# Memory products ahead of the token rows' normalisation, in one step of a hybrid decoder on one core

## The reference, cut to what matters

```python
xp = layer_norm(x_prompt, ln_in_g, ln_in_b)      # (512, 1024)
xs = layer_norm(x_sample, ln_in_g, ln_in_b)      # (8, 1024)
mkv = mem_prompt @ w_mem_kv                      # (256, 1024) @ (1024, 512): memory keys and values
z = x @ w_in                                     # x: the 520 normalised rows; 22 column tiles of 128, then 24 gate tiles
...                                              # RWKV time mixing, window attention, memory attention, gates
x1 = layer_norm(ALPHA * x + mix, ln1_g, ln1_b)
x2 = layer_norm(ALPHA * x1 + experts(x1), ln2_g, ln2_b)   # 32 experts, 2 per row

def layer_norm(x, g, b):
    mu = mean(x); var = mean((x - mu)**2)
    return (x - mu) * rsqrt(var + eps) * g + b
```

## Time and profile before

| | us |
|---|---|
| runs | 1454.42, 1457.96, 1458.41 (median 1457.96) |
| the profiled execution | 1459.9 |
| its span, first to last instruction | 1458.1 |
| TensorE busy in the span | 1163.3 (80%) |
| VectorE, ScalarE, GpSimd busy | 433.6, 239.1, 110.1 |
| mean granted clock of TensorE | 0.907 |

### The profile page before, as it was taken

The page is one execution under the profiler, slowest core; times in us unless marked ns, Lnnn a source line. Parts: engine busy times, 40 slices in busy tenths (PEclk is TensorE's granted clock), DMA queues, the critical chain, the costliest instruction groups (busy, mean ns, idle before and its releaser), DMA issues.

```text
span 1458.1 us, 22199 instructions
## 1 busy us (share of the span) xinstructions
PE 1163.3 (80%) x9283; PEld 808.1 (55%) x9283; DVE 433.6 (30%) x775; ACT 239.1 (16%) x400; POOL 110.1 (8%) x97
## 2 busy tenths in 40 slices
PE   5999989985896887898699971977878878878840
PEld 3888867774575776786585431544434434444420
DVE  5000022447464443443432236111111111111137
ACT  3100010432411111012111110211111111111101
POOL 3000000000000000000000111111111111111103
PEclk9999989998798999999799975999999999999975
DMA  7352341223033101105456222699999999999951
GB/s 265 116 149 77 76 151 45 66 65 87 1 85 85 41 29 29 43 10 182 126 152 243 109 107 62 237 427 426 425 425 419 422 416 410 421 420 420 423 216 74
DMA packets 102114, 290.91 MB, mean 200 GB/s; under 512 B 18067, under 2 KB 73429, under 8 KB 88714
## 3 DMA queue, kind: packets, MB, share of 16 engines
q1 hardware_dynamic: 96866, 281.41, 50.9%
q0 software_dynamic: 5184, 8.54, 1.7%
HBM read 274.97 MB, written 24.23 MB: 205 GB/s over the span
## 4 chain that ended last, share of the span: by engine, by line
PE 57%; DMA 25%; DVE 8%; issue 4%; SPq 2%; DVEq 2%; ACT 2%; POOL 0%; POOLq 0%; ACTq 0%
PE psum L660 54%; DMA arena<-in_e_up 12%; DMA arena<-in_e_gate 8%; DVE arena L1432 4%; PE psum L665 3%; DVE arena L1435 2%; DMA arena<-in_p_m 1%; ACT arena L1197 1%; DMA arena<-in_w_mem_kv 1%; DMA arena<-scratch_x,arena 1%; DVEq L1586 1%; SPq L584 0%; SPq L641 0%; DVEq L2014 0%; POOL arena L2027 0%
## 5 line engine op out<-in xcount | busy, mean ns | idle before, releaser
L660 PE MATMUL psum<-arena 64*64 64x64 f32 (+8 forms) x8760 | 1089.1, 344 | 178.2 <-DMA arena<-in_e_gate 61.2
L660 PEld LDWEIGHTS psum<-arena 64*64 64x64 f32 (+3 forms) x8760 | 744.9, 155 | 500.1 <-issue 251.6
L1197 ACT ACTIVATE arena<-psum 128x512 f32<-128x512 f32 (+8 forms) x151 | 94.8, 648 | 693.2 <-PE psum L660 385.8
L1432 DVE TENSOR_TENSOR arena<-arena,psum 128x256 f32<-128x256 f32 (+3 forms) x136 | 74.4, 548 | 398.3 <-PE psum L660 199.4
L1432 DVE TENSOR_TENSOR arena<-arena 128x1024 f32<-128x1024 f32 (+15 forms) x148 | 122.7, 840 | 210.5 <-PE psum L660 164.3
L665 PE MATMUL psum<-arena 128*128 128x128 f32 (+4 forms) x523 | 84.6, 302 | 64.3 <-issue 15.6
L665 PEld LDWEIGHTS psum<-arena 128*128 128x128 f32 (+4 forms) x523 | 63.6, 159 | 96.8 <-issue 65.1
L2027 POOL TENSOR_TENSOR arena<-arena 128x1024 f32<-128x1024 f32 (+1 forms) x15 | 37.1, 2476 | 578.7 <-DVE arena L1432 578.7
L1432 DVE TENSOR_TENSOR arena<-psum,arena 128x256 f32<-128x256 f32 (+5 forms) x85 | 47.4, 566 | 108.6 <-PE psum L660 107.6
L2070 POOL DMA_INDIRECT arena<-scratch_x,arena x32 | 32.8, 1024 | 300.2 <-DVE arena L1965 299.6
L1410 ACT ACTIVATE arena<-psum 128x256 f32<-128x256 f32 x32 | 12.3, 384 | 252.9 <-PE psum L660 252.9
(11 more groups left out here) (105 smaller groups left out, 155.3 us busy)
## 6 DMA issues: line engine op xcount, KB each, us to landing
arena<-in_e_gate SPq DMA_DIRECT2D x32, 2048.0 KB, 16.8
arena<-in_e_up SPq DMA_DIRECT2D x32, 2048.0 KB, 21.9
arena<-in_e_down SPq DMA_DIRECT2D x32, 2048.0 KB, 12.6
arena<-in_w_in SPq DMA_DIRECT2D x24, 512.0 KB, 4.6
arena<-in_w_in SPq DMA_DIRECT2D x44, 256.0 KB, 3.4
scratch_gates<-arena SPq DMA_DIRECT2D x24, 260.0 KB, 4.6
arena<-scratch_gates SPq DMA_DIRECT2D x8, 780.0 KB, 5.0
scratch_x<-arena SPq DMA_DIRECT2D x8, 512.0 KB
```

Of the source, the lines that this page charges most:

```text
L660: return pe.matmul(out, a, b, start=start, stop=stop)
L1197: return act.activation(out, a, ACT.Copy)
L1432: return v.tensor_tensor(out, a, b, op)
```

## The change

The memory is given transposed (`mem_T`, partition p holds the features 8p to 8p+7 for all 256 memory rows, 1024 KB), and the norm's weight and bias also as columns (`ln_in_T`, 64 bytes for each partition, 8 KB). SP's order becomes: `memT`, identity, lower half of `w_mem_kv`, row tile 0, its upper half, row tiles 1 to 4, `lnT`, the first two tiles of `w_in`, then the spread weight and bias, the constants and the rest. The queues of PE, ACT and DVE stand in this order in the diff below. TensorE makes the lower half of all memory products first, turns row tile 0, makes the upper half, and turns tiles 1 to 4. Rows are turned when scaled, without weight and bias; these are applied where the turned tile is evicted, columns 0 to 3 on DVE and 4 to 7 on ACT, one instruction a column, with weight and bias of a partition as operands. The weight and bias of the rows in `xtok` follow later (DVE, then POOL). ACT copies `mkv` after the last eviction of rows, and `mkT` is made after the tiles of `z`.

```diff
-            x_load(0)
+            sp.dma_start(memT, I["mem_T"]).then_inc(s["mem_in"], 16)
             sp.dma_start(view(C0, P + 2), I["consts"][:, 0:P + 2]).then_inc(s["ident_in"], 16)
-            sp.dma_start(gb[:, 0, :], I["ln_in_g"].partition_broadcast(P)).then_inc(s["x_in"], 16)
-            sp.dma_start(gb[:, 1, :], I["ln_in_b"].partition_broadcast(P)).then_inc(s["x_in"], 16)
-            x_load(1)
-            sp.dma_start(memtok, I["mem_prompt"].rearrange("(t p) d -> p t d", p=P)).then_inc(s["mem_in"], 16)
-            for t in range(2, Q):
-                x_load(t)
-            sp.dma_start(wmem, I["w_mem_kv"].rearrange("(p c) n -> p c n", c=KD)).then_inc(s["wmem_in"], 16)
+            sp.dma_start(wmem[:, 0:4, :], w_mem[:, 0:4, :]).then_inc(s["wmem_lo"], 16)
+            x_load(0)
+            sp.dma_start(wmem[:, 4:8, :], w_mem[:, 4:8, :]).then_inc(s["wmem_hi"], 16)
+            for t in range(1, Q):
+                x_load(t)
+            sp.dma_start(lnT, I["ln_in_T"]).then_inc(s["lnT_in"], 16)
+            p1_tile(0, 0, 1)
+            p1_tile(1, 1, 2)
+            sp.dma_start(gb[:, 0, :], I["ln_in_g"].partition_broadcast(P)).then_inc(s["x_in"], 16)
+            sp.dma_start(gb[:, 1, :], I["ln_in_b"].partition_broadcast(P)).then_inc(s["x_in"], 16)
...
             def turn_x(t):
-                pe.wait_ge(s["x_normed"], t + 1)
+                pe.wait_ge(s["x_scaled"], t + 1)
                 if t >= 2:
                     pe.wait_ge(s["xT_ready"], t - 1)
+                    pe.wait_ge(s["xT_half"], t - 1)
...
-            for t in range(2):
-                for c in range(KD):
-                    last = turn(bank(4 + 2 * t, KD, P)[:, c, :], memtok[:, t, c::KD])
-                last.then_inc(s["mem_turned"], 1)
-            pe.wait_ge(s["memT_ready"], 2)
-            pe.wait_ge(s["wmem_in"], 16)
...
+            for half in range(2):
+                pe.wait_ge(s["wmem_hi" if half else "wmem_lo"], 16)
                 for t in range(2):
+                    for c in range(half * 4, half * 4 + 4):
+                        last = mm(bank(4 + t, 512), memT[:, c, t * P:(t + 1) * P], wmem[:, c, :], c == 0, c == KD - 1)
+                    if half:
+                        last.then_inc(s["mkv_made"], 1)
+                if half == 0:
+                    turn_x(0)
+            for u in range(1, Q):
+                turn_x(u)
             pe.wait_ge(s["xT_ready"], Q)
+            pe.wait_ge(s["xT_half"], Q)
...
             def x_turned(t):
                 act.wait_ge(s["x_turned"], t + 1)
-                copy(xT[:, :, t * P:t * P + n], bank(2 * (t % 2), KD, P)[:, :, 0:n]).then_inc(s["xT_ready"], 1)
+                for c in range(KD // 2, KD):
+                    last = act.activation(xT[:, c, t * P:t * P + n], bank(2 * (t % 2), KD, P)[:, c, 0:n], ACT.Identity,
+                                          bias=lnT[:, 1, c:c + 1], scale=lnT[:, 0, c:c + 1])
+                last.then_inc(s["xT_ready"], 1)
+            act.wait_ge(s["lnT_in"], 16)
+            layer_norm(xtok, 0, 1, after=lambda t: x_turned(t - 2) if t >= 2 else None)
+            x_turned(Q - 1)
             for t in range(2):
                 act.wait_ge(s["mkv_made"], t + 1)
                 copy(mkv[:, t, :], bank(4 + t, 512)).then_inc(s["mkv_ready"], 1)
...
+            for t in range(Q + 2):
+                if t < Q:
+                    n = rows(t)
+                    v.wait_ge(s[f"tile{t}_in"], 16)
+                    for h in range(2):
+                        v.bn_stats(st6[0:n, t, h, :], xtok[0:n, t, h * 512:(h + 1) * 512])
+                    v.drain()
+                    v.bn_aggr(mv[0:n, t, :], st6[0:n, t, :, :]).then_inc(s["ln_stats"], 1)
+                u = t - 1
+                if 0 <= u < Q:
...
+                    v.reciprocal(rstd[0:n, u, :], rstd[0:n, u, :])
+                    v.drain()
+                    stt(nmr[0:n, u, :], mv[0:n, u, 0:1], -1.0, rstd[0:n, u, :], ALU.mult, ALU.mult).then_inc(s["ln_rs"], 1)
+                u = t - 2
+                if u >= 0:
+                    n = rows(u)
+                    v.wait_ge(s["x_turned"], u + 1)
...
+                    for c in range(KD // 2):
+                        last = ts(xT[:, c, u * P:u * P + n], bank(2 * (u % 2), KD, P)[:, c, 0:n], lnT[:, 0, c:c + 1], ALU.mult,
+                                  lnT[:, 1, c:c + 1], ALU.add)
+                    last.then_inc(s["xT_half"], 1)
+            v.wait_ge(s["x_in"], 32)
+            for t in range(Q):
+                n = rows(t)
+                tt(xtok[0:n, t, :], xtok[0:n, t, :], gb[0:n, 0, :], ALU.mult).then_inc(s["ln_gained"], 1)
```

More of the change, by code:

```diff
@@ L196, in build @@
         PRM = take(PR_N + 6)
+        LNT = take(2 * KD)
         GBo = take(2 * D)
@@ L216, in build @@
         gb = view(GBo, 2, D)
+        lnT = view(LNT, 2, KD)
         sm = [SMo]
@@ L245, in build @@
         xtok = view(Fo, NT + 1, D)
-        memtok = view(Fo + 5120, 2, D)
         memT = view(Fo + 7168, KD, NMEM)
@@ L434, in _ @@
             first = C0 + P + 2
[L435 to L449 removed]
             w_in = I["w_in"].rearrange("(p c) n -> p c n", c=KD)
+            w_mem = I["w_mem_kv"].rearrange("(p c) n -> p c n", c=KD)
             def p1_load(q, need, src_a, src_b, dst_a, dst_b):
@@ L468, in _ @@
             for f in range(2 * PIECES + 2):
-                p1_tile(f, f % 2, f + 1)
+                if f >= 2:
+                    p1_tile(f, f % 2, f + 1)
                 if f == 1:
@@ L715, in _ @@
                     last.then_inc(s["z_made"], 1)
+            pe.wait_ge(s["mkv_ready"], 2)
+            for f in range(2):
+                for t in range(2):
+                    last = turn(bank(6, 2, NMEM)[:, f, t * P:(t + 1) * P], mkv[:, t, f * P:(f + 1) * P])
+            last.then_inc(s["mkv_made"], 1)
             pe.wait_ge(s["z_ready"], NF + 2)
@@ L1201, in layer_norm @@
             def layer_norm(x, pas, lag, before=None, after=None):
+                scaled = s["x_scaled" if pas == 0 else "ln_scaled"]
                 for t in range(Q + lag):
@@ L1214, in layer_norm @@
                         act.activation(x[0:n, i, :], x[0:n, i, :], ACT.Identity, bias=nmr[0:n, i, :],
-                                       scale=rstd[0:n, i, :]).then_inc(s["ln_scaled"], 1)
+                                       scale=rstd[0:n, i, :]).then_inc(scaled, 1)
                     if after:
@@ L1234, in _ @@
                 copy(mkv[:, t, :], bank(4 + t, 512)).then_inc(s["mkv_ready"], 1)
[L1235 to L1238, removed]
             act.sem_inc(s["z_ready"], 2)
@@ L1244, in _ @@
                          psum[:, 2 * q:2 * q + 2, 0:NH]).then_inc(s["z_ready"], 1)
+            act.wait_ge(s["mkv_made"], 3)
+            copy(mkT, bank(6, 2, NMEM)).then_inc(s["mkT_ready"], 1)
             act.wait_ge(s["side_turned"], SIDE_PARAMS)
@@ L1462, in layer_norm @@
                         i, n = tile_at(pas, u), rows(tile_at(pas, u))
-                        v.wait_ge(s["ln_scaled"], pas * Q + u + 1)
+                        v.wait_ge(s["ln_scaled"], (pas - 1) * Q + u + 1)
                         tt(x[0:n, i, :], x[0:n, i, :], gb[0:n, 0, :], ALU.mult).then_inc(s["ln_gained"], 1)
[L1466 to L1471, removed]
+            for t in range(Q + 2):
[9 more added lines that the diff above has]
+                    n = rows(u)
+                    v.wait_ge(s["ln_std"], u + 1)
+                    v.reciprocal(rstd[0:n, u, :], rstd[0:n, u, :])
[3 more added lines that the diff above has]
+                if u >= 0:
+                    n = rows(u)
+                    v.wait_ge(s["x_turned"], u + 1)
+                    if u == 0:
+                        v.wait_ge(s["lnT_in"], 16)
+                    for c in range(KD // 2):
[6 more added lines that the diff above has]
+                tt(xtok[0:n, t, :], xtok[0:n, t, :], gb[0:n, 0, :], ALU.mult).then_inc(s["ln_gained"], 1)
             v.wait_ge(s["mkT_ready"], 1)
@@ L2131 @@
     give("x_sample", np.reshape(a["x_sample"], (B, D)))
-    give("mem_prompt", np.reshape(a["mem_prompt"], (NMEM, D)))
+    give("mem_T", np.transpose(np.reshape(a["mem_prompt"], (NMEM, P, KD)), (1, 2, 0)))
+    give("ln_in_T", np.stack([np.reshape(a[n], (P, KD)) for n in ("ln_in_g", "ln_in_b")], 1))
     give("state_wkv", np.reshape(a["state_wkv"], (B * HA, 64, 64)))
```

26 lines of the change are left out of this document (9 added, 17 removed).

## The result

The changed kernel takes 1466.59 us, median of 9 runs (1463.88 to 1471.13), against 1457.96 for 9 runs of the kernel before (1451.20 to 1463.04): ratio 1.0066, interval 1.0047 to 1.0086. It is slower, by about 8.6 us at the medians, and lies above the predicted 1460.4 us and above the range's upper end of 1464.5. The profiled execution took 1466.59 us with a span of 1464.7, 6.6 us over the span before.

A forecast was written before the change was run, and what follows sets the result against it. The prediction took the start and speed of `z`, behind `w_mem_kv` and the memory products, as the bound; -3.2 + 2.5 + 2.5 + 0.6 = +2.4 us on 1457.96 gave 1460.4 us, range 1454.5 to 1464.5.

The forecast's parts named there:

- the first one: Whole kernel: everything after `z` waits for it, so only when and how fast `z` begins matters; no size of its own.
- the rivals: Only the fall before `z`, 1457.9 us (0.22); faster head, down to 1452.9 (0.14); late `lnT`, 1462.4 to 1464.1 (0.18).
- Lower products at 9.0: Head, TensorE: lower weights land at 9.0 us, and the first half of the memory products ends at 18 to 19.
- `lnT` at 17.2: Head, load ACT first waits for: `lnT` lands at 17.2 us, between 16.0 and 18.4.
- Turning of tile 0 at 20.55: Head, TensorE: after `lnT`, table load, root, reciprocal and scaling, row tile 0 can be turned at 20.55 us.
- The fall before the upper half: Head: TensorE's pause of some 2 us drops its clock to 0.50, costing 2.5 us (zero to 3.1).
- the two readings of the transposes: Head clock: transposes don't count as work (skill's rule), making this fall sure, or do (rows), leaving a quarter chance of none.
- From T to `z`: Head, from tile 1 turned (T = 29.4 us) to `z`: alternating ACT and DVE work takes 11.1 us; `z` at 40.5, -3.2.
- The fall before `z`: Run-up to `z`: TensorE's pauses drop the clock to 0.50, all but certainly, costing 2.5 us (zero to 3.1).
- The tail of `z`: End of `z`: TensorE waits for the copy to `mkT` behind ACT's last eviction, +0.6 us (zero to 0.7).
- Sum of the head: All terms: -3.2 for `z` sooner, +2.5 and +2.5 for clock falls, +0.6 for the tail, together +2.4 us.

The follow-up runs named there:

- E5: The changed kernel with `lnT` loaded third instead of tenth and 32 do-nothing instructions at TensorE's head, later code in place: 1455.61 us, ratio 0.9990.
- E1: The changed kernel with 32 do-nothing instructions at TensorE's head, later code standing where the kernel before has it: 1457.06 us, ratio 0.9996.
- E2: The kernel before with only the memory given transposed and one do-nothing instruction, TensorE's later code 32 instructions lower: 1465.57 us, ratio 1.0049.
- E8: E6 with 97 instead of 33 do-nothing instructions at TensorE's head, later code 64 further on than in the kernel before: 1454.51 us, ratio 0.9992.
- E6: E5 plus three PSUM places, scaling before evictions, statistics before DVE's halves, turning between product quarters, `mkv` after `z_ready`; code in place: 1449.06 us, ratio 0.9936.

## Why the prediction was wrong

The step that failed is the first one: "What comes after `z` waits for it in every queue. So the question is when and how fast `z` begins." That the rest begins with `z` holds; that it then takes as long as before does not. In the profiles it took 7.4 us longer, and 8.1 us were lost in the time-mixing loop, code that the diff doesn't touch, because TensorE's program before it is 32 instructions shorter. Three pairs show it: the change with its code moved and in place (1.0066 against 0.9996 and 1.0016), the transposed memory alone (1.0049 against 1.0007), the three places in PSUM (0.9978 against 0.9936 and 0.9926), 4 to 7 per mille each time. None of the rivals had this, and none could be priced by the rows that I had read: they were of the head, of forms and of clocks.

The other steps, in their order:

- Lower products at 9.0: 8.48 us, ended at 18.1 (forecast 18 to 19). `lnT` at 17.2: 16.88. Turning of tile 0 at 20.55: 20.30. These were right.
- The fall before the upper half, 2.5 us: it came, at 20.39, and cost 1.8, as 1.97 + 7.91 us against E5's 1.05 + 7.04. It does not decide between the two readings of the transposes, for both had a fall here.
- From T to `z`, 11.1 us: 9.5, from 30.91 to 40.45. ACT's and DVE's evictions that it rests on:

```profile
30.91 1.51 ACT L1233 ACTIVATE arena<-psum,arena 128x128 f32<-128x128 f32 x4 [4.22 <-PE psum L672]
...
37.67 2.43 ACT L1233 ACTIVATE arena<-psum,arena 128x128 f32<-128x128 f32 x8
40.01 1.05 ACT L1205 ACTIVATE arena<-psum 128x512 f32<-128x512 f32 x2
```

```profile
30.91 1.36 DVE L1446 TENSOR_SCALAR arena<-psum,arena 128x128 f32<-128x128 f32 x4 [5.50 <-PE psum L672]
```

  Four columns took 1.51 on ACT (1.55 taken), the last eight 2.43 (2.75), four on DVE 1.36 (1.05). The `mkv` copies, for which the sum had 1.15 us, were not in the way: `z` began at 40.45, while they ran.
- The fall before `z`, 2.5 us: it came, and cost 156.59 - 154.72 = 1.9. The tail of `z`, +0.6: from the end of `z` to the side transposes 1.33 us instead of 0.79, +0.5.
- Sum of the head: +2.4 forecast; -0.8 in the profiles, for the `z` of 40.45 has the first fall already in it, which the sum put on top.

With its code in place the change is worth 0.9996 or 1.0016: no difference that a measurement tells. That this lies inside the predicted range is in part luck: the head came out 3.2 us better than the sum had it, and a loss that the sum did not have took most of that back. What the change gains ahead of `z` it gives back, and not only where the prediction looked. E1's `z` begins 3.4 us sooner than that of the kernel before (40.33 against 43.69); the fall of the clock in `z` and the longer tail leave 1.0 at the side transposes (198.21 against 199.20). By 365 us the lead is 2.2 us, and then the 56 products that took 24.03 us instead of 20.85, at the lower clock from their start, take it away. The prediction weighed falls of the clock only up to `z`. What makes this stretch at 0.50 longer no run settled: of all profiles only those of the kernel before, E2 and E8 have the 20.85 us. It rests on one profile of each; the mean granted clock goes the same way, 0.907 over E1's twelve runs and 0.911 over the thirty beside them, the falls of the head included. E5 and E6 name what holds it: ACT's wait for the tenth load, and evictions that alternate with the scaling.

**What the place does.** In the third pass of each kernel, from the branch that ends the second, in us: the boundary's place in the pass, the start of the block's packet in the instruction queue, and when TensorE's loads reach the boundary and go on past it.

| kernel | boundary | packet | reached | goes on |
|---|---|---|---|---|
| before | 568 | 14.7 | 25.7 | 25.7 |
| before | 824 | 27.0 | 29.9 | 29.9 |
| before | 1080 | 31.4 | 34.1 | 34.1 |
| changed | 600 | 24.5 | 25.7 | 26.9 |
| changed | 856 | 28.4 | 31.3 | 31.3 |
| changed | 1112 | 34.8 | 35.6 | 37.2 |
| E8 | 1784 | 45.3 | 46.6 | 47.7 |

In these three stops TensorE goes on 2.4 us after the packet began (to 0.1 us); in the rows where the packet began 2.7 us or more ahead of need there is none. The 2.4 us are not a fixed need: in the fourth pass of the changed kernel TensorE crosses 600 without a stop 1.9 us after the packet began. A group of 96 products takes 3.17 us, 192 instructions, so a block of these lasts 4.2 us, and little has to be late. What makes packets late is seen only in part. In the kernel before, the packet of block 568 starts at 14.7 us, while TensorE goes slowly through the loads 259 to 325 of the pass (13.0 to 21.3 us), and is there long before it is needed. In the changed kernel that of block 600 starts only at 24.5, behind this stretch and 3.4 us after TensorE has passed 344. It is so in every profile: in passes 2 to 4 this packet starts at 13.7 to 15.0 us in the seven kernels with the loop's code where the kernel before has it, and at 22.2 to 24.5 in the three with it 32 lower. But what starts a packet no run settled: that of block 568 began before TensorE's loads had reached 312, the block before it (18.4 us); and from entering a block to the next packet there were 1.3 to 1.5 us in some blocks (before, 568 and 824) and 3.4 to 3.9 in others (before, 1080; changed, 344 and 856).

## What to carry to other kernels

Here TensorE's program was fetched block by block, in a loop of 1938 instructions again in each pass; adding or removing instructions anywhere ahead of a dense stretch moves the block boundaries in it. When a change shifts time in code that it doesn't touch, look for stops without a releaser at places 256 instructions apart, and repeat the timing with fillers that put the code back, before the change itself is judged. And place fillers where the engine waits anyway: at 0.15 us each, 33 at the head cost nothing seen and 97 cost 6 us. And a lead in the profile is not yet time: a stretch at the lower clock far behind the change took some 2.5 us of it here.

## What was not expected of the hardware

TensorE's stops on its own instructions, 0.8 to 1.3 us, seven in four passes of 1938 instructions. The Trainium skill ("Runtime: NRT & Kernel Launch", section "Instruction fetch mechanics") has the next block fetched while the current one runs, and the crossing mostly hidden, since an engine issues more slowly than blocks come. By that rule the changed kernel would have no such stops in the middle of a pass. The traces here agree with the fetching, 9 to 11 packets in a pass, and not with the hiding, where 64x64 products go at 33 ns each.
